# High halves first at four run starts, the last output before the low halves, and MLA side work moved

## The reference

```
first_block, layer i:                       second_block, layer l:
  h = rmsnorm(x, g_mix); z = h @ w_in         h = rms_norm(x, norm_g); z = h @ w_in_2
  y = [MLA | short conv | 31-tap conv |       y = [fox | diff | moba | gla] attentions, gated
       retention]                             x = x + y @ w_out_2
  x = x + y @ w_o                           at the end: rms_norm(x, final_norm_g)
  u = causal conv(rmsnorm(x, g_ffn) @ w_up)
  x = x + (silu(gate) * up) @ w_down
  x = x + (p @ w_pe) * sigmoid(rmsnorm(x, g_pe) @ w_pg)
```

## Time and profile before

| | |
|---|---|
| median of 3 runs | 3499.94 us (3496.12 to 3501.02) |
| the profiled execution | 3506.58 us, its span 3504.7 us |
| TensorE busy (matmul) | 3440.0 us, 98% |
| weight loads busy | 3016.7 us, 86% |
| VectorE, ScalarE, GpSimd busy | 2624.5 (75%), 1522.9 (43%), 867.4 us (25%) |
| HBM read | 600.80 MB, 172 GB/s over the span |

### The profile page before, as it was taken

How to read it: one execution, slowest core, us unless ns; L and a number is a source line. 1 busy time by engine, 2 the same in 40 slices (tenths; PEclk the granted TensorE clock), 3 DMA queues, 4 the chain that set the end, 5 groups by cost and what they waited for, 6 DMA issues and landing times. The chain is left out here.

```text
span 3504.7 us, 55582 instructions
## 1 busy us (share of the span) xinstructions
PE 3440.0 (98%) x21166; PEld 3016.7 (86%) x21166; DVE 2624.5 (75%) x3429; ACT 1522.9 (43%) x1630; POOL 867.4 (25%) x633
## 2 busy tenths in 40 slices
PE   8999999999999999999999999999999999999998
PEld 7899888888888889998888888888888888888887
DVE  7876788787776777766887777867767766677774
ACT  5544443343333545444443433435444444444443
POOL 0332432121122423314322121213331004140004
PEclk9999999999999999999999999999999999999999
DMA  6444555454555544445555555555543445443454
GB/s 221 139 145 168 181 182 190 172 200 171 201 178 183 181 168 151 143 162 184 182 189 173 201 175 198 177 189 184 171 166 134 156 168 181 173 157 132 157 177 148
DMA packets 90073, 605.25 MB, mean 173 GB/s; under 512 B 10000, under 2 KB 10160, under 8 KB 28592
## 3 DMA queue, kind: packets, MB, share of 16 engines
q1 hardware_dynamic: 88992, 599.83, 49.9%
q10 hardware_dynamic: 912, 3.11, 0.2%
HBM read 600.80 MB, written 2.10 MB: 172 GB/s over the span
## 5 line engine op out<-in xcount | busy, mean ns | idle before, releaser
L557 PE MATMUL bank<-H,whi 128*128 128x512 f32 x6784 | 2411.2, 400 | 26.0 <-DVE H L1535 19.6
L561 PE MATMUL bank<-H,wlo 128*128 128x256 f32 x7552 | 2121.3, 281 | 0.0
L1061 ACT ACTIVATE whi<-raw 128x2048 fp32r<-128x2048 f32 (+1 forms) x610 | 1095.0, 1796 | 1133.5 <-DMA raw<-in_slabs_down 263.1
L557 PEld LDWEIGHTS bank<-H,whi 128*128 128x128 f32 x6784 | 1276.2, 188 | 347.8 <-issue 20.5
L1480 DVE TENSOR_TENSOR wlo<-raw,whi 128x2048 fp32r<-128x2048 f32 (+1 forms) x610 | 1327.8, 2177 | 186.6 <-ACT whi L1061 182.8
L561 PEld LDWEIGHTS bank<-H,wlo 128*128 128x128 f32 x7552 | 1431.4, 190 | 0.6
L557 PE MATMUL bank<-G,whi 128*128 128x512 f32 x1408 | 496.2, 395 | 0.0
L477 POOL TENSOR_TENSOR sqtmp<-tmp 128x256 f32<-128x256 f32 x88 | 219.0, 2489 | 880.3 <-DVE tmp L2052 880.3
L561 PE MATMUL bank<-G,wlo 128*128 128x256 f32 x1408 | 396.4, 282 | 0.0
L557 PEld LDWEIGHTS bank<-G,whi 128*128 128x128 f32 x1408 | 264.6, 188 | 63.3
L561 PEld LDWEIGHTS bank<-G,wlo 128*128 128x128 f32 x1408 | 264.2, 188 | 0.0
(11 more groups left out here) (334 smaller groups left out, 2450.8 us busy)
## 6 DMA issues: line engine op xcount, KB each, us to landing
raw<-in_slabs_up SPq DMA_DIRECT2D x176, 1024.0 KB, 4.9
raw<-in_slabs_down SPq DMA_DIRECT2D x128, 704.0 KB, 4.0
raw<-in_slabs_wo SPq DMA_DIRECT2D x32, 1024.0 KB, 4.9
raw<-in_slabs_pg SPq DMA_DIRECT2D x32, 1024.0 KB, 4.9
raw<-in_slabs_gates SPq DMA_DIRECT2D x32, 1024.0 KB, 4.9
raw<-in_slabs_wout SPq DMA_DIRECT2D x32, 1024.0 KB, 4.9
raw<-in_slabs_sc SPq DMA_DIRECT2D x24, 1024.0 KB, 4.9
raw<-in_slabs_fox SPq DMA_DIRECT2D x24, 1024.0 KB, 4.9
```

Of the source, the lines that this page charges most:

```text
L557: pe.matmul(b[0:r.m, :], whi[:, n % RAW, w], r.src[:, k, :], start=at == 0, stop=False)
L561: last = pe.matmul(b[0:r.m, 0:T], wlo[:, n % RAW, w], r.src[:, k, 0:T], start=False, stop=at == r.kt - 1)
L1061: act.activation(whi[:, n % RAW, 0:w], raw[:, n % RAW, 0:w], ACT.Copy).then_inc(S("hi_ready"), 1)
```

## The change

1. high_first on TensorE: in zq of layer 1, both wo, the first up group of both layers and both gla, the first two slabs are computed in two passes. First, for slab 0 and then 1, whi and wlo times the 256 high columns of all chunks (waits h_hi); then, for slab 0 and 1, whi times the low columns (waits h_ready). Slab_done of both, norm_sum and side work come after both. wo gets head = 1 (its first four slabs written out, not looped).
2. VectorE's run: the last output is emptied before all 16 low halves, not after 12 of them.
3. both_units: unit 0 takes the banks in order first + p, each waiting only for the slab that had that bank. The waits of pg's first slabs and ScalarE's and VectorE's reads follow.
4. Side work: the split of p is moved from s = 12 and 13 to the start, before the first reciprocal, with two pieces of setup(); p's load is issued ahead of the constants'. setup_end() stands at s = 31, key_rope at s = 15. Taps: 5, 3, 3 per cfa slab (was 5, 5, 5), 4 per sc slab (was 3).

```diff
-        if key[0] == "pg" or key[0] == "up" and key[2] == 0:
+        if key[0] in ("pg", "wo") or key[0] == "up" and key[2] == 0:
             by[key].head = 1
@@ TensorE
+        def high_first(key, h_base, order):
             r = by[key]
+            rank = list(range(r.kt)) if order is None else [order.index(c) for c in range(r.kt)]
+            chunks = list(range(r.kt)) if order is None else order
+            for u in range(2):
+                n = r.first + u
+                pe.wait_ge(S("lo_ready"), n + 1)
+                if n >= 4:
+                    pe.wait_ge(S("evac"), n - 3)
+                b = bank[n % 4]
+                for k in chunks:
+                    if u == 0:
+                        pe.wait_ge(S("h_hi"), h_base + rank[k] + 1)
+                    w = slice(k * r.m, (k + 1) * r.m)
+                    pe.matmul(b[:, 0:T], whi[:, n % RAW, w], r.src[:, k, 0:T], start=k == chunks[0], stop=False,
+                              skip_group_check=True)
+                    pe.matmul(b[:, 0:T], wlo[:, n % RAW, w], r.src[:, k, 0:T], start=False, stop=k == chunks[-1],
+                              skip_group_check=True)
+            for u in range(2):
+                n = r.first + u
+                b = bank[n % 4]
+                for k in chunks:
+                    if u == 0:
+                        pe.wait_ge(S("h_ready"), h_base + rank[k] + 1)
+                    last = pe.matmul(b[:, T:2 * T], whi[:, n % RAW, k * r.m:(k + 1) * r.m], r.src[:, k, T:2 * T],
+                                     start=k == chunks[0], stop=k == chunks[-1], skip_group_check=True)
+                last.then_inc(S("slab_done"), 1)
+
+        def run(key, operand=None, beside=None, base=None, free=None, order=None, high=None):
+            if high is not None:
+                high_first(key, high, order)
+                advance(beside, 4)
+                if base is not None:
+                    for u in range(2):
+                        (behind_first if key[0] in STAGES else after_slab)(key[1], base + u)
...
@@ both_units
-                        pe.wait_ge(S("evac"), r.first - 1 + min(p, 1))
-                    b = aux[p] if u else bank[(r.first + 2 + p) % 4]
+                        pe.wait_ge(S("evac"), r.first - 3 + p)
+                    b = aux[p] if u else bank[(r.first + p) % 4]
@@ the runs on TensorE
-            run(("zq", l), h_ready(hbase), None, 0)
+            run(("zq", l), h_ready(hbase), None, 0, high=hbase if l else None)
-            run(("wo", l), y_ready(hbase, 0), order=Y_ORDER[0])
+            run(("wo", l), y_ready(hbase, 0), order=Y_ORDER[0], high=hbase)
-                    run(("up", l, g), h_ready(hbase) if g == 0 else None, norm_beside() if g == 0 else None)
+                    run(("up", l, g), None, norm_beside() if g == 0 else None, high=hbase if g == 0 else None)
-            run(("pg", l), h_ready(hbase), gate_norm(l), free=lambda j, l=l: pe.wait_ge(S("pe_taken"), 6 * l + 1 + min(j, 2)))
+            run(("pg", l), h_ready(hbase), gate_norm(l), free=lambda j, l=l: pe.wait_ge(
+                *((S("pe_taken"), 6 * l + 3) if j != 1 else (S("evac"), by["pe", l].first + 1))))
-            run(("gla", l), h_ready(hbase), norm_beside(), 0)
+            run(("gla", l), None, norm_beside(), 0, high=hbase)
@@ ScalarE set_up (s = 12), and the start
             act.activation(lamv[:, 4:8], lamv[:, 0:4], ACT.Exp).then_inc(S("lam_exp"), 1)
-            act.wait_ge(S("p_in"), 16)
-            act.activation(pT_hl[:, :, :, 0:T], z[:, 16:20, :].rearrange("p (l c) t -> p l c t", l=L),
-                           ACT.Copy).then_inc(S("p_hi"), 1)
...
         split_hi(r0, 0, 3, 0)
+        act.wait_ge(S("p_in"), 16)
+        act.activation(pT_hl[:, :, :, 0:T], z[:, 16:20, :].rearrange("p (l c) t -> p l c t", l=L),
+                       ACT.Copy).then_inc(S("p_hi"), 1)
         norm()
@@ VectorE run
-                if handing:
-                    last(0, 12)
                 dve.wait_ge(S("slab_done"), r.first + j + 4 * i + 1)
                 yield i, j, bank[(r.first + j) % 4]
-                if handing:
-                    last(12, DC)
+                if last is not None and isinstance(i, int) and 4 * i + j == r.count - 1:
+                    last(0, DC)
@@ VectorE after_first, setup_end, start
-            if l == 0 and s == 13:
+            if l == 0 and s == 31:
                 setup_end()
-            if s == 13:
+            if s == 15:
                 key_rope(l)
...
-            dve.wait_ge(S("p_hi"), 1)
-            for k in range(4):
-                hl = pT_hl[:, k // 2, k % 2, :]
-                dve.tensor_tensor(hl[:, T:2 * T], z[:, 16 + k, :], hl[:, 0:T].bitcast(F32),
-                                  ALU.subtract).then_inc(S("p_ready"), 1)
-            dve.wait_ge(S("trig"), 1)
...
         split_lo(r0, 0, 3, 0)
+        advance(setting, 2)
+        dve.wait_ge(S("p_hi"), 1)
+        for k in range(4):
+            hl = pT_hl[:, k // 2, k % 2, :]
+            dve.tensor_tensor(hl[:, T:2 * T], z[:, 16 + k, :], hl[:, 0:T].bitcast(F32),
+                              ALU.subtract).then_inc(S("p_ready"), 1)
         inverse()
@@ taps
-                    advance(taps, 5)
+                    advance(taps, 5 if c == 1 else 3)
-                advance(taps, 3)
+                advance(taps, 4)
```

More of the change, by code:

```diff
@@ L533, in nth @@
             return cnt[name]
-        def run(key, operand=None, beside=None, base=None, free=None, order=None):
+        def high_first(key, h_base, order):
             r = by[key]
+            rank = list(range(r.kt)) if order is None else [order.index(c) for c in range(r.kt)]
[24 more added lines that the diff above has]
+        def run(key, operand=None, beside=None, base=None, free=None, order=None, high=None):
+            r = by[key]
+            if high is not None:
[4 more added lines that the diff above has]
+                        (behind_first if key[0] in STAGES else after_slab)(key[1], base + u)
             for i, j in groups(pe, r, 0):
+                if high is not None and isinstance(i, int) and 4 * i + j < 2:
+                    continue
                 n = r.first + j
@@ L1377, in _ @@
         x_hi("g_mix", 0, "x_in", 0)
+        act.dma_start(z[:, 16:20, :].rearrange("p a t -> p (a t)"), d["p"]).then_inc(S("p_in"), 16)
         act.dma_start(cst[:], d["const"]).then_inc(S("const_in"), 16)
@@ L1421, in _ @@
                     act.wait_ge(S("pe_out"), 6 * l + 3 * u + p + 1)
-                    b = aux[p] if u else bank[(by["pe", l].first + 2 + p) % 4]
+                    b = aux[p] if u else bank[(by["pe", l].first + p) % 4]
                     act.activation(z[:, 8 * u + 2 * p:8 * u + 2 * p + 2, :].rearrange("p a t -> p (a t)"), b[:],
@@ L1485, in run @@
             for i, j in groups(dve, r, AHEAD):
-                handing = last is not None and isinstance(i, int) and 4 * i + j == r.count - 1
-                if handing:
-                    last(0, 12)
                 dve.wait_ge(S("slab_done"), r.first + j + 4 * i + 1)
                 yield i, j, bank[(r.first + j) % 4]
-                if handing:
-                    last(12, DC)
+                if last is not None and isinstance(i, int) and 4 * i + j == r.count - 1:
+                    last(0, DC)
                 if base is not None:
@@ L2058, in _ @@
             for i, j, _ in run(("pe", l)):
-                b = pX if j else bank[(by["pe", l].first + 5) % 4]
+                b = pX if j else bank[(by["pe", l].first + 3) % 4]
                 dve.tensor_copy(z[:, 8 * j + 6:8 * j + 8, :].rearrange("p a t -> p (a t)"), b[:]).then_inc(S("evac"), 1)
```

1 line of the change is left out of this document (removed).

## The result

The changed kernel ran in 3478.51 us (median of 5 runs, 3471.88 to 3481.12), beside 3500.62 us for the kernel before on the same chip (5 runs, 3496.12 to 3501.32): ratio 0.9935, 95% interval 0.9921 to 0.9949. Run again with the later experiments it took 3475.58 us (5 runs) against 3497.89 (11 runs): 0.9937 (0.9924 to 0.995). So it is 22 us faster, where 3476 us, some 24 less, were forecast. The profiled execution took 3471.88 us, the fastest of its five, with a span of 3469.8 us; the one before had 3506.58.

A forecast was written before the change was run, and what follows sets the result against it. TensorE, busy 98% of the span, bounds the kernel, so only its delays count. Terms sum to -30.8 us, plus 6.8 for slow stretches: -24.0 from 3506.58, so 3482.6 profiled and 3476 us median; range 3462 to 3489.

The forecast's parts named there:

- Down to pg: Two places, pe units to pg: wait for last down output goes, VectorE's split 1.6 us late; -15.2 us with slow clock.
- rival C: Pe units gain little: ScalarE's banks or pg's first low split come much later; 3484 us, chance 0.07.
- Zq and gla: Zq of layer 1, gla of layer 0: slab 3 at 19.9 us, against 23.5; -7.2 together; gla of layer 1: 0.
- Up: Wo to up, two places: slab 3 starts at 19.4 us against 18.96, root's table taken as loaded early; +0.9 us together.
- Wo: Rg to wo, two places: high pass arrives earlier at the same late chunk 12; +0.9 us each, +1.8 together.
- MLA: Work leaves VectorE's queue before kv: -4.5 and -3.2 us of clock in layer 0, -2.0 and -1.7 in layer 1.
- Start: Split of p and setup pieces before the first reciprocal, 5.4 us in 5.15 us idle: +0.3, between 0 and 1.5.
- Rival D: Weight path binds in high_first at 0.188 us per product, deciding from 0.153: slower, 3524 us, chance 0.04.
- the new slow stretches: New waits in wo (2.3 us and more) and up (2.1) bring low clock: four of 1.7 us, +6.8.
- Rival B: No new wait reaches the clock, and each MLA's two later slow stretches go or shrink: 3466 us, chance 0.14.
- Rival A: Clock takes it back: nine new waits bring slow stretches, and up's root table waits too; 3487 us, chance 0.18.

The follow-up runs named there:

- undone in one experiment: The changed kernel without high_first in wo, which is computed in one pass with its loop as before: 3472.96 us (4 runs), ratio 0.9914.
- avoided in another: The changed kernel with wo's high pass in four parts, the last four chunks of both slabs last: 3472.35 us (6 runs), ratio 0.9929.
- second profile: Profile of the changed kernel run once more with no edit: 3475.58 us (5 runs), profiled execution the median one; ratio 0.9937 to the kernel before.
- parts 2 and 3 alone: Kernel before with only the last output emptied before all low halves and the new bank order: 3492.43 us (6 runs), ratio 0.9966.

## Why the prediction was right, point by point

*Down to pg*: right, by the mechanism named. The lateness is 1.0 us and not 1.6, since the 16 low halves took 7.26 us and not 7.8. Single rows of the changed kernel say why:

```profile
1139.81 0.83 DVE L1570 SCALAR_TENSOR_TENSOR H<-x,cols,H 128x256 fp32r<-128x256 f32 x1
1140.57 0.96 DVE L1570 SCALAR_TENSOR_TENSOR H<-x,cols,H 128x256 fp32r<-128x256 f32 x1
1141.45 0.47 DVE L1570 SCALAR_TENSOR_TENSOR H<-x,cols,H 128x256 fp32r<-128x256 f32 x1
...
1139.58 0.79 POOL L450 TENSOR_TENSOR sqtmp<-x 128x256 f32<-128x256 f32 x1 [0.27 <-DVE x L1589]
1140.44 0.80 POOL L455 TENSOR_TENSOR sqacc<-sqacc,sqtmp 128x256 f32<-128x256 f32 x1
```

A low half alone takes 0.40 us from start to start (thirteen such steps from 1141.45 to the split at 1146.60), the two beside GpSimd 0.76 and 0.88. So the two GpSimd operations cost 0.36 + 0.48 = 0.84 us, as the 0.8 of the forecast. What was mis-sized is the 0.44 of the earlier trace rows: the first of its twelve lay beside the end of a GpSimd operation too, and a slowed low half was counted once too often.

```profile
1150.31 0.95 DVE L1535 SCALAR_TENSOR_TENSOR H<-x,cols,H 128x256 fp32r<-128x256 f32 x1
...
1148.18 2.79 POOL L455 TENSOR_TENSOR sqacc<-sqacc,sqtmp 128x256 f32<-128x256 f32 x1
```

The lock between the two engines that the Trainium skill describes (SBUF — State Buffer, Who interferes with whom) would have allowed 1.6; these rows show half of that. They agree with a lock in that each slowed low half ends some 0.3 us behind the GpSimd operation beside it (1140.64 behind 1140.37, 1141.53 behind 1141.24). The banks that ScalarE reads did not bind, so rival C is out.

*Zq and gla*: the norm's chain is 1258.10 - 1250.43 = 7.67 us against 7.6 worked out, slab 3 at 19.77 against 19.9. Up: 7.86 against 7.9, 19.38 against 19.4. The root's table is loaded ahead of ScalarE's wait, as taken:

```profile
401.39 1.28 ACT L1126 ACT_TABLE_LOAD   x1
406.51 0.48 ACT L1126 ACTIVATE rms<-pX,eps 128x256 f32<-128x256 f32 x1 [3.84 <-PE pX L638]
```

*Wo*: a loss of 0.8 and 0.9 us per place, +0.9 forecast; undone in one experiment and avoided in another. *MLA*: right in layer 0; in layer 1 the kv wait and the stretch behind it went too, but the excess fell by 0.7 less than worked out, and why is open. The two later stretches of each MLA stayed in the first profile, as the sum had taken. *Start*: the pieces took 5.2 us beside the forecast 5.4; the reciprocal stands at 34.21, 0.27 later than in the earlier trace rows, and nothing waited longer for it than the 1.25 us of before.

*Rival D* is out: from the first high product to the norm's in up, 96 products take 11.52 us, 0.120 us each, against 0.117 forecast and the 0.153 from which it decides. That is 0.3 us per place.

*The step that failed* is the sum's last term, the new slow stretches: four of 1.7 us forecast, none in the first profile, one in the second. Two mistakes put the four above the mark. One is of scale: I compared new waits, counted as lateness against the pace (2.3 in wo, 2.1 in up), with idle times that the profile lists (1.95 with a slow stretch, 1.40 without). The list counts idle time from the end of the last product's record, and that record (0.28 us) goes on 0.16 us past the point at which the next product would have started (0.12). The other is of size: in wo of layer 0 the high half of chunk 12 came 4.95 us after the run's start (301.33) and not 5.1, and in up the norm's product and slab 2 took 6.09 us, not 5.8. Together they make listed waits of 1.91 and 1.79 in wo, 1.62 and 1.61 in up: up well below the 1.95 and not above it, wo just under it. And the single row of 1.95 was no mark to go by. Over the ten profiles of this study the listed waits of 1.40 us and more, without the first and the last of each, fall so:

| listed idle time, place | times | followed by products at 1.2 GHz |
|---|---|---|
| 1.40 to 1.72, wlo at a slab's start | 25 | 0 |
| 1.40 to 1.52, H, both halves in one pass, in up, gla, wo and wout | 5 | 1 |
| 1.75 to 1.91, wo's H | 8 | 2 |
| 1.84 to 1.95, kv of layer 1 | 3 | 3 |
| 2.20 to 6.41, H, kv of layer 0, last down output | 17 | 17 |

Rival B had the total of the profile (-34 forecast, -34.7 us in the profiled executions) but only half of the mechanism. No new wait reached the clock; the later stretches of each MLA stayed in both layers (in the second profile those of layer 1 were gone), and what made up for them is down to pg, zq, gla and set-up, 3.2 us better than their rows of the forecast. Rival A fits none of the runs. Why two of wo's eight waits are followed by the slow clock and six are not, and one of three equal waits of 1.46 us, I did not settle; all three are in layer 1, so what ran ahead of the wait may count.

The prediction also says that the profile stamps slow stretches some 10 us late. It does not: in the trace before the granted clock is 0.57 over 1360 to 1364, where the products are slow, and 1.00 over 1364 to 1368. No term hung on it.

*Why the median fits all the same.* I carried the 6.64 us by which the profiled execution before stood above its median over to the changed kernel. It did not hold: the changed kernel's first profiled execution stood 6.63 us below its median, the second at it. So two errors nearly cancel: the profiled execution was forecast 10.7 us too slow (3482.6, measured 3471.88), 6.8 of it the clock's term, and its distance to the median was 13.3 us off. That the median came out within 2.5 us is luck. The kernel's runs differ by their clock: of 27 runs of the kernel before, the nine at 0.990 average 3502.9 us and the ten at 0.992 3497.8; ten runs of the changed kernel have a mean of 0.9949, those 27 one of 0.9912. By these means (0.9949 - 0.9912) x 3,490 = some 13 of the 22 us are clock, by estimate, and how much varies from run to run.

## What to carry to other kernels

A pass that uses early data first moves its wait only as far as the producer of the late data lets it: change the producer's order in the same edit, and look at what the pass pushes back (here the norm's product, 2 us in five places, free again once it stood between the passes). Compare a worked-out lateness with a listed wait only on one scale; the list starts at the end of the last record. Take the price of an operation from single rows where another engine runs beside some of them; the mean of a merged row hides which were slowed. And an offset between one profiled run and the median is no constant to carry over to a kernel whose waits differ.

## What the runs showed of the hardware

- Products at 1.2 GHz followed all 17 listed waits of 2.20 us and more and 1 of 30 between 1.40 and 1.72 us; between these both kinds stand (table above). Equal waits of one kernel differed (1.46 us with parts 2 and 3 alone, one of three), and stretches at 1.2 GHz came and went between two profiles of the same kernel (MLA of layer 1). In wo of layer 1 it fell 1.4 us after the wait was over (products at 0.28 from 1525.39 to 1526.65, at 0.42 from 1526.93).
- VectorE's low half of 256 columns took 0.40 us alone and 0.76 and 0.88 us beside GpSimd operations of 0.8; the subtraction of p's low half took 1.43 / 4 = 0.36 us each in set-up, where GpSimd was idle, and 0.78 in the earlier trace rows.
- 256-column products that each load their weights ran at 0.120 us in high_first, with whi loaded twice per chunk, against 0.117 in the earlier trace rows.
